# A two-layer decoder step: raw rows transposed ahead of the norm, router logits by token, and a routing table of row numbers for the first 128 places

## The chip, the cores and the metric

The kernel runs on one core of one Trainium2 chip. The metric is the device time of one execution in microseconds (us); lower is better. The engines are TensorE (PE in the rows, PEld for its weight loads), VectorE (DVE), ScalarE (ACT), GpSimd (POOL) and SyncE (SP), which here only issues DMA transfers.

## The reference

One step of a decoder with 2 layers and a model width of 1024, over 512 prompt tokens and 64 sample tokens (8 sequences of 8). Only what the change touches:

```python
def rmsnorm(x, g):
    return x * lax.rsqrt(jnp.mean(x * x, axis=-1, keepdims=True) + RMS_EPS) * g

def mixer_block(x, ...):
    z = rmsnorm(x, norm_g) @ w_in          # 1024 -> 2560: u | q | k | v | g
    ...                                    # pooling mixer on u, retention on q, k, v, gate g
    return x + concat([pool_out, ret_out]) @ w_out

def hier_moe(x, ...):
    hf = rmsnorm(x, norm_g)
    grp_logits = hf @ w_rg + b_rg          # 4 groups
    exp_logits = hf @ w_re + b_re          # 16 experts, 4 in a group
    # best group by logit, the best two experts in it; gates by softmax
    # y = sum over experts e of gates[:, e] * (silu(hf @ w_gate[e]) * (hf @ w_up[e])) @ w_down[e]
    return x + y
```

After the second layer a last RMSNorm gives the outputs. All arrays are float32.

## The kernel before

**Tiling.** The 576 tokens are 5 tiles of 128 (the last, `LAST`, holds the 64 sample tokens). `x` stays on chip, tokens on partitions. A product with float32 accuracy is made of three TensorE passes: each operand is split into a high part, rounded by ScalarE to the fast float32 form, and a low part that VectorE subtracts, and high*high, high*low and low*high are summed. So `hT`, `lT` are the two parts of the transposed activations, `wh`, `wl` those of a weight tile of 128x512 that arrives in `raw`. `w_hi` and `w_lo` make the parts of a weight tile, 56 of them in a layer (steps `s`): 40 of `w_in`, 16 of `w_out`. A step is 14 matmuls of 128x512 (three for each full tile of tokens, two for the last, whose parts lie side by side), for all five tiles of tokens, and TensorE goes through the steps without a pause where nothing is missing. Steps 0 to 2 go tile by tile, since they start while the tiles are still being normed; the last four steps of `w_out` do too.

**Norm ahead of a product** (`norm_root`, `norm_hi` on ScalarE, `norm` and `norm_lo` on VectorE, `transposes` on TensorE). For each tile: ScalarE squares the row and takes the root, VectorE takes the reciprocal and multiplies x by it and by the gain row (`xm` ahead of the mixer and at the end, `xf` ahead of the experts), TensorE transposes the result in two halves of four 128x128 blocks, ScalarE writes the high part and VectorE the low part of each half.

**Banks of w_in.** The products of a group of 512 columns lie in 6 PSUM banks (`ZB`) for 5 tiles; a bank is copied out (`z_evac`) by ScalarE for the tiles LAST, 0, 2, and by VectorE for 1, 3, before the second tile of the next group may use bank 0.

**Routing** (`logits`, `routing`). After the norm ahead of the experts the 20 router logits are formed with the weights (`wrs`, high and low part side by side, 40 columns) as the stationary operand, in two halves of 320 tokens, then turned back to tokens on partitions by five small transposes. VectorE then runs a chain of small operations: best group, best two experts of it, the place of each token in its expert's list (`place_of`, from a matmul with a triangle of ones), and a table that gives for each expert and each place the number of the row. The table is built for all five turns of 128 places (`atslot`, `spread`, ten matmuls, and seven operations after them that end with `pidx` and `tidx`). The normed rows `xf` go to memory (`xn_d`), and GpSimd gathers for each expert the rows by `tidx` with an indirect DMA; after the expert the rows are scattered to `y_d` by `pidx`. Each expert's list here fits the first 128 places, and the code for later turns is jumped over.

**Experts.** 16 experts in order, each 24 matmuls of 128x512 for gate and up, 12 for down, and ten transposes; the weights of experts 0, 1, 2 are loaded during the end of `w_out`; those of expert 3 (`AHEAD`, 3 MB in four transfers) into buffers that the norm and the router still use, so that SyncE waits for the writes of `xn_d` and for the logits ahead of it. Afterwards the rows of `y_d` come back as `back` (ten transfers, two for each tile), and `combine` adds them to `x` with the gates `pgate`.

## Time and profile before

| | |
|---|---|
| median of 3 runs | 933.63 us (933.05 to 934.26) |
| the profiled execution's own time | 933.09 us |
| its span, first to last instruction | 931.3 us |
| TensorE busy | 801.2 us, 86% of the span |
| VectorE busy | 637.5 us, 68% |
| ScalarE busy | 459.7 us, 49% |
| GpSimd busy | 258.9 us, 28% |
| chain that ended last | TensorE 81%, VectorE 10%, DMA 4%, ScalarE 3%, issue 2% |
| moved by DMA | 184.64 MB, mean 198 GB/s |

An engine's busy share is a mean over stages. The two layers are told apart by time: layer 0 ends where the rows of its experts are added (about 447 us), layer 1 about 900 us. The chain that ended last is followed back from the last instruction, at each step to what released it.

### The profile page before, as it was taken

The numbers are of one execution on the slowest core, as the hardware profiler recorded it, in microseconds if no ns is written. First come the engines' busy times: TensorE is split into PE (matmuls) and PEld (weight loads), VectorE is DVE, ScalarE is ACT, GpSimd is POOL, SyncE is SP. The second block draws the span as 40 slices with busy tenths as digits, with TensorE's granted clock in tenths as the row PEclk, the third lists the DMA queues.
The fourth block names the chain that finished last, engine by engine and source line by source line (L and its number), as shares of the span: only waits on it lengthen the run. The fifth ranks groups of instructions, "written<-read, shape, count | busy, mean of one in ns | idle before, by whom it ended". The sixth has DMA issues, their size and how long they took to land.

```text
span 931.3 us, 11658 instructions
## 1 busy us (share of the span) xinstructions
PE 801.2 (86%) x3974; PEld 656.7 (71%) x3974; DVE 637.5 (68%) x1009; ACT 459.7 (49%) x767; POOL 258.9 (28%) x211
## 2 busy tenths in 40 slices
PE   5999999999827999998199999999994499999930
...
GB/s 293 156 69 77 74 72 81 80 135 209 398 145 191 315 315 396 395 347 89 249 83 140 71 73 70 79 112 26 168 376 294 77 313 288 373 387 377 208 132 200
DMA packets 61356, 184.64 MB, mean 198 GB/s; under 512 B 15452, under 2 KB 17756, under 8 KB 52970
## 3 DMA queue, kind: packets, MB, share of 16 engines
...
q14 instruction: 22, 0.18, 0.1%
...
## 4 chain that ended last, share of the span: by engine, by line
PE 81%; DVE 10%; DMA 4%; ACT 3%; issue 2%; SPq 0%; POOLq 0%; ACTq 0%; DVEq 0%
PE ps L368 13%; PE ps L372 10%; PE ps L371 10%; PE ps L1043 10%; PE ps L1045 10%; PE ps L1044 10%; PE ps L1049 3%; PE ps L370 3%; DVE x L1590 2%; PE ps L1225 2%; PE ps L1217 1%; DVE xm L1483 1%; DMA back<-y_d 1%; PE ps L1038 1%; DVE x L1367 1%
## 5 line engine op out<-in xcount | busy, mean ns | idle before, releaser
L368 PE MATMUL ps<-wh,hT 128*128 128x512 f32 x480 | 193.8, 404 | 4.3 <-ACT z L821 2.4
L1498 DVE TENSOR_TENSOR wl<-raw,wh 128x512 fp32r<-128x512 f32 x112 | 95.6, 859 | 112.2 <-ACT wh L811 112.0
L1504 DVE TENSOR_TENSOR gul<-wgu,eh 128x1024 fp32r<-128x1024 f32 x128 | 150.8, 1218 | 10.0 <-ACT eh L836 9.7
L372 PE MATMUL ps<-wh,lT 128*128 128x512 f32 x384 | 151.2, 394 | 0.0
L371 PE MATMUL ps<-wl,hT 128*128 128x512 f32 x384 | 151.1, 393 | 0.0
L811 ACT ACTIVATE wh<-raw 128x512 fp32r<-128x512 f32 x112 | 69.7, 630 | 140.2 <-PE ps L370 111.5
L836 ACT ACTIVATE eh<-wgu 128x1024 fp32r<-128x1024 f32 x128 | 128.9, 1057 | 10.5 <-PE ps L1045 10.5
L1043 PE MATMUL ps<-eh,hgTh 128*128 128x512 f32 x256 | 104.5, 408 | 6.2 <-DVE hgTl L1515 6.2
L368 PEld LDWEIGHTS ps<-wh,hT 128*128 128x128 f32 x480 | 91.0, 190 | 25.5 <-issue 8.0
L1045 PE MATMUL ps<-eh,hgTl 128*128 128x512 f32 x256 | 101.3, 396 | 0.0
L1044 PE MATMUL ps<-gul,hgTh 128*128 128x512 f32 x256 | 101.2, 395 | 0.0
...
L372 PEld LDWEIGHTS ps<-wh,lT 128*128 128x128 f32 x384 | 72.9, 190 | 15.9
L371 PEld LDWEIGHTS ps<-wl,hT 128*128 128x128 f32 x384 | 73.2, 191 | 13.5
L1509 DVE TENSOR_TENSOR dnl<-wdn,eh 128x1024 fp32r<-128x1024 f32 x64 | 75.5, 1222 | 2.5 <-ACT eh L845 1.9
L656 POOL DMA_INDIRECT hg<-xn_d,tidx x32 | 38.0, 1188 | 133.8 <-PE ps L1049 106.2
L845 ACT ACTIVATE eh<-wdn 128x1024 fp32r<-128x1024 f32 x64 | 64.3, 1061 | 0.0
L1043 PEld LDWEIGHTS ps<-eh,hgTh 128*128 128x128 f32 x256 | 48.9, 191 | 17.3 <-DVE hgTl L1515 7.5
L1043 PE MATMUL ps<-eh,actTh 128*128 128x512 f32 x128 | 54.0, 422 | 6.1 <-DVE dnl L1509 6.1
L1045 PEld LDWEIGHTS ps<-eh,hgTl 128*128 128x128 f32 x256 | 48.8, 191 | 10.7
L1044 PEld LDWEIGHTS ps<-gul,hgTh 128*128 128x128 f32 x256 | 49.0, 191 | 9.4
L850 ACT ACTIVATE hgTh<-ps 128x512 fp32r<-128x512 f32 x64 | 34.8, 596 | 40.8 <-PE ps L1049 40.8
...
## 6 DMA issues: line engine op xcount, KB each, us to landing
...
```

Of the source, the lines that this page charges most:

```text
L368: pe.matmul(out, both, w_h, start=first, stop=False)
L371: pe.matmul(out, both, w_l, start=False, stop=False)
L372: return pe.matmul(out, l[:, t * P:(t + 1) * P], w_h, start=False, stop=final)
L811: sc.activation(wh[S % SPL][:, :], raw[S % RAW][:, :], ACT.Copy).then_inc(whi, 1)
L836: sc.activation(eh[p][:, :], gu_pair(wgu, wgu3, e, s, p), ACT.Copy).then_inc(ghi, 1)
L845: sc.activation(eh[4 + k][:, :], dn_chunk(wdn, wdn3, e, s, k), ACT.Copy).then_inc(dhi, 1)
L1043: pe.matmul(out, hi_l, hi_r, start=first, stop=False)
L1044: pe.matmul(out, hi_l, lo_r, start=False, stop=False)
L1045: return pe.matmul(out, lo_l, hi_r, start=False, stop=final)
L1498: ve.tensor_tensor(wl[S % SPL][:, :], raw[S % RAW][:, :], wh[S % SPL][:, :].bitcast(F32), ALU.subtract).then_inc(wlo, 1)
L1504: ve.tensor_tensor(gu_pair(gul, gul3, e, s, p), gu_pair(wgu, wgu3, e, s, p), eh[p][:, :].bitcast(F32), ALU.subtract).then_inc(glo, 1)
L1509: ve.tensor_tensor(dn_chunk(dnl, dnl3, e, s, k), dn_chunk(wdn, wdn3, e, s, k), eh[4 + k][:, :].bitcast(F32), ALU.subtract).then_inc(dlo, 1)
```

## The change

**The norm of the mixer.** TensorE transposes `x` itself (`mix_rows`), so a tile can be transposed as soon as it is there. The gain (`gcol`, one column of 128 numbers for each block) is multiplied into `w_in` while its parts are made, in `w_hi` and `w_lo`; the squares and one root for all tiles (`mix_square`, `mix_root`) run during the steps 3 to 8, and `rstd` is applied where the PSUM banks are copied out (`z_evac`, `z_last`).

**The norm ahead of the experts.** `x` is transposed (`ffn_rows`) into `xT`, plain float32 without a low part. The squares are taken in two halves of the row. The normed rows `xf` (`xn_rows`) are now only for the gather; those of the last tile are made late, in the middle of `routing`. The logits are formed by token, `xT` stationary and the 20 columns of `wr` (with the gain multiplied in) moving, in plain float32, five times 8 matmuls. The bias is multiplied by `rms` in place of dividing the logits (`bias_scale`), and the scale `rstd` comes in only ahead of the two exponentials.

**Routing.** The tests for the best use differences against zero. The table is built for the first 128 places only, as row numbers right away (`name_p` and `name_b`, 20 matmuls of 32 columns, one operation that writes `rowidx`); what later turns need stands in `later_turns`, inside the branch that is not taken here. The last norm is as before. SyncE no longer loads the gain of the mixer's norm.

```diff
-            load_x(0)
-            load_gain(0)
-            for t in range(1, NT):
+            sp.dma_start(gcol[:, :, :, :], a["gcol"]).then_inc(gcol_ld, 16)
+            for t in range(NT):
                 load_x(t)
-                if t - 1 < RAW:
-                    load_raw(0, t - 1)
+                if t < RAW:
+                    load_raw(0, t)
...
-                load_gain(2 * L + 2)
+                if L + 1 == NL:
+                    load_gain(NL)
                 for t in (2, 3, LAST):
                     sp.wait_ge(xn_st[t], 16 * (L + 1))
-                sp.wait_ge(lg_mm, L + 1)
+                sp.wait_ge(lg_mm, 2 * (L + 1))
...
+            def mix_square(L, t):
+                x_there(sc, L, t)
+                sc.activation(xn[0][t][:, :], x[:, t, :], ACT.Square, accum_out=ss[:, t:t + 1]).then_inc(sq_done, 1)
+            def mix_root(L):
+                sc.wait_ge(sq_done, 16 * L + NT)
+                sc.activation(rms[:, :], ss[:, :], ACT.Sqrt, bias=eps[:, 0:1], scale=1.0 / D).then_inc(rms_done, 1)
...
+            def ffn_square(L, t, half):
+                sc.wait_ge(xw, 15 * L + NT * (1 + half) + t + 1)
+                if half == 0 and t >= 3:
+                    sc.wait_ge(s0_st, 64 * (L + 1))
+                cols = slice(512 * half, 512 * half + 512)
+                sc.activation(xn[1][t][:, cols], x[:, t, cols], ACT.Square, accum_out=(ss, ss2)[half][:, t:t + 1]).then_inc(sq_done, 1)
...
+            def ffn_root(L, t):
+                sc.wait_ge(sq_done, 16 * L + 2 * NT + t + 2)
+                sc.activation(rms[:, t:t + 1], ss2[:, t:t + 1], ACT.Sqrt, bias=ssb[:, t:t + 1], scale=1.0 / D).then_inc(rms_done, 1)
+            def ffn_rows(L, t):
+                sc.wait_ge(tr_done, 20 * L + 10 + 2 * t + 1)
+                if t == 0:
+                    sc.wait_ge(s0_st, 64 * (L + 1))
+                sc.activation(xT[:, 0:4, t * P:(t + 1) * P], tr_bank(1, 2 * t).rearrange("p (k c) -> p k c", k=4), ACT.Copy).then_inc(hi_done, 1)
+            def xn_out(L, t):
+                sc.wait_ge(xn_done, NT * L + t + 1)
+                sc.dma_start(xn_d[t * P:(t + 1) * P, :], xn[1][t][:, :]).then_inc(xn_st[t], 16)
...
-                sc.activation(wh[S % SPL][:, :], raw[S % RAW][:, :], ACT.Copy).then_inc(whi, 1)
+                if s < WIN_STEPS:
+                    sc.activation(wh[S % SPL][:, :], raw[S % RAW][:, :], ACT.Copy, scale=gcol[:, 0, L, s % KC:s % KC + 1]).then_inc(whi, 1)
...
+                    if m == LAST or (m == 0 and g == 0):
+                        sc.wait_ge(rstd_done, L + 1)
...
+                    sc.activation(dst, ps[m % ZB][:, :], func, scale=rstd[:, t:t + 1]).then_inc(z_part if t == LAST else zfree[m % ZB], 1)
...
+                table(ACT.Sqrt)
+                for t in range(NT):
+                    mix_hi(L, t)
+                    if L == 0:
+                        for s in ((0, 1), (2,), (), (), ())[t]:
+                            w_hi(0, s)
                 for s in range(RAW, WIN_STEPS + 3):
                     w_hi(L, s)
+                    if s - RAW < NT:
+                        mix_square(L, s - RAW)
+                    if s - RAW == NT:
+                        mix_root(L)
...
-                norm(2 * L + 1)
+                for t in range(NT):
+                    ffn_square(L, t, 0)
+                ffn_first_half(L)
+                for t in range(NT):
+                    if t < LAST:
+                        ffn_square(L, t, 1)
+                        ffn_root(L, t)
+                    ffn_rows(L, t)
+                    if t and t < LAST:
+                        xn_out(L, t - 1)
+                ffn_square(L, LAST, 1)
+                ffn_root(L, LAST)
+                xn_out(L, 3)
                 table(ACT.Exp)
...
-            def logits(L, i):
-                pe.wait_ge(wr_lo, L + 1)
-                pe.wait_ge(lo_done, 10 * (2 * L + 1) + (6, 10)[i])
...
+            def logits(L, t):
+                out = ps[0][:, 20 * t:20 * t + 20] if t < LAST else ps[7][0:NSAMP, 0:20]
+                pe.wait_ge(wr_g, L + 1)
+                pe.wait_ge(hi_done, 15 * L + 10 + t + 1)
                 for k in range(KC):
-                    if k:
-                        pe.matmul(out[0:20, 0:n], wrs[:, k, 0:20], lT[:, k, low], start=False, stop=False)
-                    last = pe.matmul(out[0:40, 0:TOK // 2], wrs[:, k, :], hT[:, k, cols], start=(k == 0), stop=(k == KC - 1))
-                    if k == 0:
-                        pe.matmul(out[0:20, 0:n], wrs[:, k, 0:20], lT[:, k, low], start=False, stop=False)
-                last.then_inc(lgT_mm, 1)
+                    if k == 4:
+                        pe.wait_ge(lo_done, 15 * L + 10 + t + 1)
+                    last = pe.matmul(out, xT[:, k, t * P:t * P + tokens(t)], wr[:, k, :], start=(k == 0), stop=(k == KC - 1))
...
-                for t in range(NT + 2):
-                    if t < NT:
-                        for s in range(2 * KC - SPL, 2 * KC):
-                            wout_mm(L, s, t)
-                    if t == NT + 1:
-                        logits(L, 0)
-                    if t >= 2:
-                        transposes(2 * L + 1, t - 2)
-                logits(L, 1)
...
                 for t in range(NT):
-                    last = pe.transpose(ps[3][:, 40 * t:40 * t + 40], lgT[0:40, t * P:(t + 1) * P], ident[0:40, 0:40])
-                last.then_inc(lg_mm, 1)
+                    for i in range(2 * KC - SPL, 2 * KC - 2):
+                        wout_mm(L, i, t)
+                    if t == LAST:
+                        logits(L, 2)
+                    for i in range(2 * KC - 2, 2 * KC):
+                        wout_mm(L, i, t)
+                    if t:
+                        ffn_rows(L, t - 1)
+                    if t in (2, 3):
+                        logits(L, t - 2)
+                ffn_rows(L, LAST)
+                logits(L, 3)
+                logits(L, LAST)
...
-                pe.wait_ge(tab_ready, L + 1)
                 for i in range(2 * NT):
-                    last = pe.matmul(ps[2][:, 0:NT * 2 * NE], atslot[:, i, :], spread[:, i, :], start=(i == 0), stop=(i == 2 * NT - 1))
+                    if i % NT == 0:
+                        pe.wait_ge(tab_ready, 2 * L + i // NT + 1)
+                    pe.matmul(ps[2][:, 0:2 * NE], atslot[:, i, :], over(name_p[:, i, :], 2), start=(i == 0), stop=False)
+                    last = pe.matmul(ps[2][:, 0:2 * NE], atslot[:, i, :], name_b[:, i, :, :], start=False, stop=(i == 2 * NT - 1))
                 last.then_inc(tab_mm, 1)
...
+            ve.tensor_tensor(name_p[:, :, :], one, c("pair", 2 * NT)[:, :, 0:1].to_broadcast([P, 2 * NT, NE]), ALU.mult)
+            ve.tensor_tensor(name_b[:, :, :, :], over(one, 2, 2), c("block", 2 * NT).unsqueeze(3).to_broadcast([P, 2 * NT, 2, NE]), ALU.mult)
+            ve.wait_ge(pos_mm, L + 1)
+            link(ve.tensor_tensor(picked[:, :, :, :], both[:, :, :, :], over(ps[1][:, 0:NT * NE].rearrange("p (t e) -> p t e", t=NT), 2), ALU.mult))
+            link(ve.tensor_reduce(place_of[:, :], picked[:, :, :, :].rearrange("p k t e -> p (k t) e"), AX.X, ALU.add))
+            for k in range(2):
+                half = slice(NT * k, NT * k + NT)
+                ve.tensor_tensor(atslot[:, half, :], over(c("slot"), NT), place_of[:, half].unsqueeze(2).to_broadcast([P, NT, P]),
+                                 ALU.is_equal).then_inc(tab_ready, 1)
+            link(ve.tensor_reduce(most_f[:, :], ps[1][:, 96:96 + NE], AX.X, ALU.max))
+            xn_rows(L, LAST)
+            link(ve.tensor_tensor(gds[:, :, :], gd[:, :, :], wide(rstd[:, :], 4), ALU.mult))
+            ve.tensor_tensor(col(4), col(2), rstd[:, :], ALU.mult).then_inc(exp_in, 1)
+            ve.wait_ge(tab_mm, L + 1)
+            ve.tensor_scalar(rowidx[:, :, :], ps[2][:, 0:2 * NE].rearrange("p (w e) -> p w e", w=2), float(NO_ROW), None, ALU.add).then_inc(tidx_done, 1)
...
+            def ffn_rows(L, t):
+                ve.wait_ge(tr_done, 20 * L + 10 + 2 * t + 2)
+                ve.tensor_copy(xT[:, 4:8, t * P:(t + 1) * P], tr_bank(1, 2 * t + 1).rearrange("p (k c) -> p k c", k=4)).then_inc(lo_done, 1)
+            def ffn_scale(L, t):
+                ve.wait_ge(rms_done, 6 * L + 2 + t)
...
+            def xn_rows(L, t):
+                if t == 0:
+                    ve.wait_ge(gain_ld, 16 * (L + 1))
+                ve.scalar_tensor_tensor(out=xn[1][t][:, :], in0=x[:, t, :], scalar=rstd[:, t:t + 1], in1=gain[:, :],
+                                        op0=ALU.mult, op1=ALU.mult).then_inc(xn_done, 1)
+            def bias_scale(L):
+                link(ve.tensor_tensor(brms[:, :, :], over(rbias[:, :], NT), rms[:, :].unsqueeze(2).to_broadcast([P, NT, 20]), ALU.mult))
...
-                    norm(2 * L, lambda t, k: combine(L - 1, t, k))
+                    combine(L - 1, 0, 0)
+                    combine(L - 1, 0, 1)
                 else:
-                    norm(0)
+                    ve.wait_ge(gcol_ld, 16)
+                for t in range(NT):
+                    if L and t + 1 < NT:
+                        combine(L - 1, t + 1, 0)
+                    mix_lo(L, t)
+                    if L and t + 1 < NT:
+                        combine(L - 1, t + 1, 1)
+                    if L == 0:
+                        for s in ((0, 1), (2,), (), (), ())[t]:
+                            w_lo(0, s)
+                if L == 0:
                     ve.wait_ge(cst_ld, 32)
                 for s in range(RAW, WIN_STEPS + 4):
                     w_lo(L, s)
+                    if s == RAW + NT + 1:
+                        mix_scale(L)
...
-                norm(2 * L + 1, lambda t, k: None if k else x_add(ve, L, 2, t))
-                routing(ve, L, link, gu_lo)
+                x_add(ve, L, 2, 0)
+                for t in range(3):
+                    x_add(ve, L, 2, t + 1)
+                    ffn_rows(L, t)
+                    ffn_scale(L, t)
+                    xn_rows(L, t)
+                x_add(ve, L, 2, LAST)
+                ffn_rows(L, 3)
+                ffn_rows(L, LAST)
+                ffn_scale(L, 3)
+                xn_rows(L, 3)
+                ffn_scale(L, LAST)
+                bias_scale(L)
+                routing(ve, L, link, gu_lo, xn_rows)
```

How the instructions stand on an engine, before and after, at three places.

VectorE at the start of layer 1, where the experts' rows are added to x (`back_*` are the loaded rows, `xm_*` the normed tile). Before:

```order
L1590 SCALAR_TENSOR_TENSOR x<-back_114,pgate,x 128x1024
L1590 SCALAR_TENSOR_TENSOR x<-back_115,pgate,x 128x1024
L1482 RECIPROCAL rstd<-rms 128x1
L1483 SCALAR_TENSOR_TENSOR xm_169<-x,rstd,gain 128x1024
L1590 SCALAR_TENSOR_TENSOR x<-back_116,pgate,x 128x1024
L1469 TENSOR_TENSOR lT<-ps,hT 128x4x128 x2
```

The same place after the change:

```order
L1706 SCALAR_TENSOR_TENSOR x<-back_116,pgate,x 128x1024
L1561 TENSOR_TENSOR lT<-ps,hT 128x4x128 x2
L1706 SCALAR_TENSOR_TENSOR x<-back_117,pgate,x 128x1024
L1706 SCALAR_TENSOR_TENSOR x<-back_118,pgate,x 128x1024
L1561 TENSOR_TENSOR lT<-ps,hT 128x4x128 x2
```

The reciprocal and the multiplication by `rstd` and the gain have left the stretch; two additions and one pair of low parts for each tile stay.

TensorE at the end of layer 0's `w_out`, without the rows of `w_out` itself (`xf_*` normed tiles; the name ahead of the comma is the moving operand, the other the stationary one). Before, the last rows up to the table:

```order
L1038 MATMUL ps<-cst,xf_177 128x128 x8
...
L1156 MATMUL ps<-hT,wrs 40x320
L1306 MATMUL ps<-cst,lgT 128x40 x5
L1312 MATMUL ps<-taken,tri 128x16 x15
L1315 MATMUL ps<-taken,tri 128x16 x5
L1320 MATMUL ps<-spread,atslot 128x160 x10
```

After the change:

```order
L1225 MATMUL ps<-wr,xT 128x20 x8
L385 MATMUL ps<-wh_62,hT 128x512
L387 MATMUL ps<-wl_66,hT 128x512
L385 MATMUL ps<-wh_63,hT 128x512
L387 MATMUL ps<-wl_67,hT 128x512
L1100 MATMUL ps<-cst,x 128x128 x16
L1225 MATMUL ps<-wr,xT 128x20 x8
L1225 MATMUL ps<-wr,xT 64x20 x8
L1381 MATMUL ps<-taken,tri 128x16 x15
L1385 MATMUL ps<-taken,tri 128x16 x5
```

Three of the five tiles' logits now stand inside the last steps of `w_out`, and behind the last step there are 16 transposes and 16 small matmuls where there were 24 transposes, 32 matmuls of 192 or 320 columns and five small transposes.

VectorE in `routing` of layer 0, from the places to the row numbers (`L1504` and `L1619` are the low parts of expert 0's weights). Before:

```order
L1427 TENSOR_REDUCE place_of<-picked 128x10
...
L1432 TENSOR_TENSOR atslot<-cst,in_turn 128x1280
L1433 TENSOR_TENSOR spread<-hotturn,named 128x1600
...
L1448 TENSOR_SCALAR small_tab<-tmpf 128x80
L1449 TENSOR_TENSOR tidx<-small_tab,tmpf 128x80
L1504 TENSOR_TENSOR gul_74<-wgu_68,eh_121 128x1024
```

After the change:

```order
L1492 TENSOR_REDUCE place_of<-picked 128x10
L1495 TENSOR_TENSOR atslot<-cst,place_of 128x640 x2
L1497 TENSOR_REDUCE most_f<-ps 128x1
L1584 SCALAR_TENSOR_TENSOR xf_186<-x,rstd,gain 128x1024
L1499 TENSOR_TENSOR gds<-gd,rstd 128x20
L1500 TENSOR_TENSOR small<-small,rstd 128x5
L1503 TENSOR_SCALAR rowidx<-ps 128x32
```

Fifteen operations from the places to the row numbers have become seven, and one of the seven is the last tile of normed rows, which before stood well ahead of `routing`.

## Rows read from the trace of the kernel before

**Rows 1.** Stretches: engine busy us and instructions, granted clock, DMA share, GB/s

```profile
28.20:124.00 95.80, 94.04 (x424) 75.82 (x423) 43.83 (x62) 29.70 (x63) 43.83 (x35) 1.00 0.35 97
...
230.60:246.90 16.30, 15.66 (x80) 12.52 (x78) 13.77 (x22) 8.68 (x19) 0.00 (x0) 1.00 1.01 413
246.90:284.60 37.70, 12.76 (x92) 9.55 (x91) 26.11 (x69) 12.71 (x22) 7.83 (x7) 0.68 0.53 196
284.60:437.50 152.90, 148.30 (x716) 122.45 (x716) 142.72 (x169) 123.40 (x169) 37.18 (x27) 0.99 0.82 305
```

**Rows 2.** Timeline of the start: start us, us, engine, line, operation, count

```profile
4.65 1.06 ACT L776 ACTIVATE xm<-x 128x1024 f32<-128x1024 f32 x1 [2.40 <-DMA x<-in_x_prompt]
...
7.13 1.28 DVE L1483 SCALAR_TENSOR_TENSOR xm<-x,rstd,gain 128x1024 f32<-128x1024 f32 x1
8.18 1.06 ACT L776 ACTIVATE xm<-x 128x1024 f32<-128x1024 f32 x1 [2.06 <-DMA x<-in_x_prompt]
...
11.09 1.28 DVE L1469 TENSOR_TENSOR lT<-ps,hT 128x512 fp32r<-128x512 f32 x2
...
13.88 0.77 PE L368 MATMUL ps<-wh,hT 128*128 128x512 f32 x1 [0.62 <-DVE wl L1498]
...
18.83 0.48 PE L368 MATMUL ps<-wh,hT 128*128 128x512 f32 x1
```

**Rows 3.** Timeline of TensorE where step 3 begins, layer 0

```profile
28.21 0.39 PE L368 MATMUL ps<-wh,hT 128*128 128x512 f32 x1
28.44 0.39 PE L371 MATMUL ps<-wl,hT 128*128 128x512 f32 x1
```

**Rows 4.** Timeline of layer 1's start

```profile
455.65 1.29 DVE L1590 SCALAR_TENSOR_TENSOR x<-back,pgate,x 128x1024 f32<-128x1024 f32 x1 [1.76 <-DMA back<-y_d]
...
458.48 1.94 PE L1038 MATMUL ps<-cst,xm 128*128 128x128 f32 x8 [16.36 <-DVE xm L1483]
...
477.14 1.03 PE L1038 MATMUL ps<-cst,xm 128*128 128x128 f32 x8
...
481.52 0.39 PE L368 MATMUL ps<-wh,hT 128*128 128x512 f32 x1
```

**Rows 5.** Timeline where the second group of w_in begins, layer 0

```profile
44.77 1.08 ACT L821 ACTIVATE unat<-ps 128x512 f32<-128x512 f32 x2
...
45.51 0.47 PE L368 MATMUL ps<-wh,hT 128*128 128x512 f32 x1 [0.59 <-ACT unat L821]
```

**Rows 6.** Line L889: ScalarE copies of a PSUM bank with a scale for each partition

```profile
L889 ACT ACTIVATE hP<-ps,pscale x8: 687/687/689, 62.8 to 564.6; 128x512 fp32r<-128x512 f32 x8
```

**Rows 7.** Line L821: who waited for these copies, us and times

```profile
  PE ps L368: 3.5, 6
```

**Rows 8.** Timeline of layer 0 from the last tiles of w_out to expert 0

```profile
249.61 1.57 PE L1038 MATMUL ps<-cst,xf 128*128 128x128 f32 x8 [2.67 <-DVE xf L1483]
...
260.63 0.17 DVE L1392 TENSOR_REDUCE small<-lg 128x5 f32<-128x20 f32 x1
...
265.48 0.24 DVE L1411 TENSOR_TENSOR taken<-picked,cst 128x80 bf16<-128x80 f32 x1
...
268.71 1.49 DVE L1432 TENSOR_TENSOR atslot<-cst,in_turn 128x1280 bf16<-128x1280 f32 x1
...
274.87 0.24 DVE L1449 TENSOR_TENSOR tidx<-small_tab,tmpf 128x80 uint32<-128x80 f32 x1
...
275.98 1.24 POOL L656 DMA_INDIRECT hg<-xn_d,tidx  x1 [13.18 <-DVE tidx L1449]
...
280.59 1.97 PE L1049 MATMUL ps<-cst,hg 128*128 128x128 f32 x8 [7.08 <-DMA hg<-xn_d,tidx]
...
284.64 0.79 PE L1043 MATMUL ps<-eh,hgTh 128*128 128x512 f32 x1 [2.09 <-DVE hgTl L1515]
```

**Rows 9.** The chain that ended last: 16 float32 matmuls with 128x128 weights, 8 columns each

```profile
183.06 1.69 PE ps L1217 x16
```

**Rows 10.** Writes of the last outputs (L1005), issue to landing, ns and us

```profile
L1005 ACTq DMA_DIRECT2D out_y_prompt<-xm x4: 338/342/351, 913.3 to 926.0; - x4
...
DMA to landing us min/median/max: 2.6/2.8/3.8
```

**Rows 11.** The gathers (L656), issue to landing over both layers

```profile
DMA to landing us min/median/max: 4.7/7.5/8.8
```

**Rows 12.** The loads of back (L593), issue to landing

```profile
DMA to landing us min/median/max: 3.4/7.4/11.4
```

294 lines of the change are left out of this document (153 added, 141 removed).

## The prediction

> **What bounds the kernel now.** I read the stretches first [rows 1]. From 28.2 to 124 us and from 284.6 to 437.5 us TensorE works for 97 to 98% of the time: there it sets the pace, and a change of other engines' work is worth nothing unless it makes TensorE wait. In 230.6 to 246.9 us it is at 15.7 of 16.3 us. The stretch behind it is different: of 37.7 us TensorE works 12.8, at a granted clock of 0.68. This is where the norm, the router and the first gather stand one behind the other, once in each layer. The timelines show the other two places, the start [rows 2] and the start of layer 1 [rows 4]. The last norm is a fourth, but its order on each engine stays, so it adds nothing. The sum is therefore over two starts and two routing stretches, less what the steps of `w_in` lose.
>
> **The start of layer 0.** Tile 0 of x is there at 4.65 us (its square starts), the normed tile is ready at 7.13 + 1.28 = 8.4, and only then can TensorE transpose it; the first product starts at 13.88 and step 3 at 28.21 [rows 2, 3]. Afterwards x itself is transposed. One small load (`gcol`) goes ahead, so say tile 0 at 5.2. The gain row's 512 KB leave the queue, so tile 1, which landed by 8.2, comes at about 7.3. Transposes at the low clock take 1.94 for eight [rows 4]: tile 0 to 7.2, tile 1 to 9.3. The parts of weight tile 0 stand behind tile 0's parts, ready about 9.4, and the first product starts there, 4.4 earlier. The third weight tile's low part stands behind the low parts of tile 1 (1.28 for two [rows 2]), at about 12.0, when TensorE needs it. From then on it is TensorE's work as before: two tiles' starts stood 2.95 apart. Step 3 starts at about 24.0. Gain **4.2**. If the loads are the limit, only half: 2; if everything shifts by the first product, 4.4.
>
> **The start of layer 1.** The additions for tile 1 wait for `back` until 455.65, and step 3 starts at 481.52 [rows 4]. In between VectorE has per tile two additions (2.4), the multiplication (1.3), a reciprocal (0.2) and a pair of low parts (1.3): 5.1. Without the two middle ones it is 3.7 for a tile. TensorE has 1.03 of transposes and nine matmuls, 2.05 at the cadence of 0.227 us for one [rows 3], so 3.1 at the full clock: VectorE stays the slower, but for the first tile, where TensorE is at the low clock. Walking it through: additions to 456.9, low parts of tile 0 to 458.2, then one tile in about 3.7 to 4.4, last addition at 471.5, last transposes 472.5, tiles 3 and 4 of the products 2.05 + 1.36, step 3 at 475.9. Gain **5.6**. The ten loads of `back` land 3.4 to 11.4 after their issue [rows 12], a spread of 8 us over five tiles, so they are not in the way of a pace of 3.7. Bounds: 3.5 if the low clock lasts a tile longer, 6.5 if it is four times 1.5 and a little.
>
> **The steps of w_in.** The scale in the bank copies: ScalarE's copy with a scale per partition takes 0.687 [rows 6] against 0.54 to 0.6 now (two in 1.08) [rows 5], and TensorE waits for the second of two such copies, 0.59 us [rows 5], in all 3.5 us at six places [rows 7]. Two copies 0.09 longer make each wait 0.18 longer: loss **1.1**. The scale in `w_hi` (0.09 more) and in `w_lo` (one row of the same kind is 1.28 for 1024 columns, so 0.65 to 0.7 for 512, as now) lies under steps of 14 x 0.227 = 3.2 us, and so do the squares moved to steps 3 to 7: ScalarE then has 0.7 + 1.3 = 2.0 of 3.2. Without that cover each square would cost its 1.3. The root is ready two steps before the first bank is to be copied.
>
> **The routing stretch.** TensorE's last steps start at 230.6. Now 56 matmuls (12.7), eight transposes for a tile (0.9) and the logits. Float32 matmuls with 128x128 weights and few columns: 16 in 1.69 [rows 9], so 0.85 for a tile's eight. From below a transposing group of eight costs no less; from above it would be the double, at the low clock. Placed in the order shown, the last `w_out` matmul ends at 249.1, the last addition to x at 250.5, the last transposes at 251.5, the last logits at 253.2. There VectorE has been behind: additions 1.35, copy, copy, `xf` of tile 3 (1.28), two reciprocals, the bias, two additions of the logits, done at 254.6. Before, this point is 260.63 [rows 8], because TensorE waited 2.67 for a normed tile and then did 32 wide matmuls, half of them at the low clock. Gain so far 6.0.
>
> From there to `taken`: before 260.63 to 265.72 with 23 operations, now 20 at 0.21 and a few longer ones, 4.5: 259.1. From there to `place_of`: 0.4 + 0.3 + 0.5 + 0.7 = 2.0. `atslot` in halves costs its 1.49 once [rows 8], `spread` (1.8) and nine of the small operations are gone. But behind `atslot` stands `xf` of the last tile: most_f 0.2, then 1.28, so the row is ready at 264.1, and `rowidx` at 264.6, against `tidx` at 275.1. That is 10.5 earlier.
>
> **The new wait.** The gather needs `xn_d` complete. Before, all normed rows were made ahead of the logits, so the write lay far ahead of the gather. Now it is issued at 264.1. Writes of 512 KB with nothing else going on take 2.6 to 3.8, median 2.8 [rows 10]: 267.0. The gather starts 0.87 behind its release, as now (275.11 to 275.98), at 267.9. Queued behind the write are GpSimd's gathers and, on SyncE, the four loads for expert 3, 3 MB, which wait for the same semaphore. So these start together with the first gather. Before, they were released by the logits' end, some 15 us ahead of the gather, and that gather took 275.98 to 280.59, 4.6 [rows 8]; over both layers gathers take 4.7 to 8.8, median 7.5 [rows 11]. I take 7.5, since the median is that of gathers beside weight loads. So the rows are there at 275.4 instead of 280.59: gain **5.2** in layer 0. Expert 0 then takes its 4.05 as before [rows 8], the high and low parts of its weights being ready by 271.7. In layer 1 the gain row of the last norm is loaded at the moment of the last `xn_d` write, since SyncE waits for all `xf` ahead of it; 512 KB beside it cost about 1.0: gain **4.2**.
>
> The Trainium skill (DMA: Bandwidth & Descriptors, Anatomy of one DMA) gives a fixed 2.0 us and the bytes at 436 per ns for one transfer: an estimate of 3.2 us for this write. The trace's median for the same thing is 2.8 [rows 10]. By the page the gain would be 0.8 us smaller over two layers; the sum goes by the row.
>
> **Sum.** 4.2 + 5.6 - 1.1 + 5.2 + 4.2 = 18.1 us. The profiled execution took 933.09, so 915.0; the median of the runs is 0.5 above it: **915.5 us**. The experts' loops, 153 us each, neither gain nor lose.
>
> **Rivals.**
> 1. *The gather is not slowed.* The rows of a gather may get their share beside the loads: it takes 4.7, and the write in layer 1 isn't slowed either. Then 2 x 2.8 + 1.0 = 6.6 more: 909. For it: the loads' first bytes and the gather's start within a microsecond of each other, and 512 KB are small. Against: the `xn_d` writes beside loads and the gathers inside the loop are all slowed.
> 2. *The starts give less.* The loads at the start (x and three weight tiles) and the low clock in layer 1 hold TensorE back, or VectorE's chain ahead of the logits, which has some 20 us of work in 23, slips by a microsecond or two. Half of both starts gone (4.9) and 1 in each routing stretch: 922.
> 3. *Slower: the two trips to memory in a row.* The write of the last `xf` and the gather that needs it now stand on the path. Each may take as long as the longest landing of 512 KB in the trace, 11.4 [rows 12]. Then rows come at 264.1 + 11.4 + 0.9 + 11.4 = 287.8, 7.2 later than before in each layer, and with the starts' gain of 8.7 the time is 939. It decides from a sum of 19.9 us for both trips; I expect 10.3. Against it: the 11.4 is a load last of ten in a queue, and at 264 us nothing else is queued.
> 4. *No change.* Transposing x earlier could be of no use if the weights' parts came last at both starts, and routing's saving went into the wait for `xn_d`. That wants a trip sum of about 16 and starts of nothing: 933.
>
> **How the numbers follow.** Chances: forecast 0.50, rival 1 0.26, rival 2 0.17, no change 0.03, rival 3 0.04. The forecast's own range is 912 to 919 (start 2 to 4.4, layer 1 3.5 to 6.5, gather 6.5 to 8.8 with each layer). The range 908 to 922 takes in rivals 1 and 2. A measurement tells some 0.2% (1.9 us) from no change: faster 0.93, within 0.03, slower 0.04.
>
> **What the profile after would show.** Step 3 at about 24 us; TensorE's share of the first 28 us up. The bank waits six times 0.77 instead of 0.59. The logits 8 in 0.85 and the first reduce at 254.6. `rowidx` ten us ahead of the old `tidx`, but the first gather released by the landing of `xn_d`, not by VectorE, about 268, and its landing 7 to 8 us later, with wgu and wdn loads under way. In layer 1 VectorE's additions without a pause from 455.65 less the shift, 3.7 for a tile. The prediction is wrong if the gather starts at 265.5 (the write doesn't hold it), if its landing is 4.7, if VectorE falls behind TensorE's logits by more than 2 us, or if TensorE waits in the steps 3 to 10 of a layer for `wl` or `rstd`.

## The result, and the profile after

The changed kernel took **927.17 us** (median of 8 runs, 924.59 to 933.80), the kernel before in the same session 934.14 (8 runs, 933.05 to 935.56): ratio **0.9937**, 95% interval 0.9909 to 0.9965. The sign of the forecast is right, its size is not: 7.0 us were won where 18.1 had been forecast, and the time lies 5 us above the upper end of the range. The profiled execution took 927.14, with a span of 925.3 against 931.3.

The stretches of the changed kernel come first (same columns as [rows 1], same places of the program; the last row is layer 1's experts).

```profile
23.00:119.00 96.00, 93.69 (x423) 75.61 (x423) 44.07 (x63) 36.88 (x72) 43.67 (x35) 1.00 0.35 97
226.10:243.50 17.40, 17.19 (x103) 14.45 (x101) 12.45 (x20) 9.52 (x27) 0.00 (x0) 1.00 0.99 399
243.50:280.10 36.60, 14.09 (x123) 12.31 (x123) 21.19 (x56) 10.26 (x17) 8.49 (x7) 0.63 0.50 181
280.10:439.53 159.43, 153.24 (x728) 125.89 (x728) 144.37 (x170) 124.31 (x171) 41.82 (x28) 0.98 0.79 296
729.49:890.98 161.49, 155.31 (x728) 127.48 (x728) 144.74 (x170) 124.87 (x171) 37.44 (x27) 0.96 0.77 286
```

From the last steps of `w_out` to expert 0 it was 16.3 + 37.7 = 54.0 us [rows 1] and is 17.4 + 36.6 = 54.0. The stretch that should have become some 5 us shorter is as long as it was. TensorE works 10% more in it (17.19 + 14.09 = 31.3 us against 15.66 + 12.76 = 28.4), and its granted clock in the second part went from 0.68 to 0.63.

Next the two starts (timeline; they answer to [rows 2 to 4]): the first product and step 3 of layer 0, then the first additions and step 3 of layer 1.

```profile
9.49 0.78 PE L385 MATMUL ps<-wh,hT 128*128 128x512 f32 x1
...
23.06 0.39 PE L385 MATMUL ps<-wh,hT 128*128 128x512 f32 x1
...
447.14 2.67 DVE L1706 SCALAR_TENSOR_TENSOR x<-back,pgate,x 128x1024 f32<-128x1024 f32 x2 [5.10 <-DMA back<-y_d]
...
471.97 0.39 PE L385 MATMUL ps<-wh,hT 128*128 128x512 f32 x1
```

Step 3 of layer 0 stands at 23.06, before at 28.21: 5.15 won. In layer 1 it comes 24.83 behind the first additions, before 30.30 (451.22 to 481.52): 5.47 won. Twelve kernels of this study have these two starts, and their profiles differ: step 3 of layer 0 stands between 22.89 and 24.32 (once at 26.92), that of layer 1 comes 24.83 to 26.43 behind the first additions. This profile has the shortest of the twelve starts of layer 1. In the steps behind them, line L857 (the bank copies, now with a scale) has these users, to be read beside [rows 7]:

```profile
L857 ACT ACTIVATE z<-ps,rstd x28: 670/684/693, 68.1 to 613.2; 128x512 f32<-128x512 f32 x28
...
  PE ps L385: 4.6, 6
```

And the way to expert 0 in layer 0 (timeline, to be read beside [rows 8]):

```profile
253.97 0.18 DVE L1464 TENSOR_REDUCE small<-lg 128x5 f32<-128x20 f32 x1
...
258.17 0.24 DVE L1478 TENSOR_TENSOR taken<-ohg,ing 128x80 bf16<-128x80 f32 x1
...
261.89 1.28 DVE L1584 SCALAR_TENSOR_TENSOR xf<-x,rstd,gain 128x1024 f32<-128x1024 f32 x1
...
263.20 0.33 ACTq L830 DMA_DIRECT2D xn_d<-xf  x1
263.38 0.18 DVE L1503 TENSOR_SCALAR rowidx<-ps 128x32 uint32<-128x32 f32 x1
...
265.95 0.80 SPq L504 DMA_DIRECT2D wgu<-in_gate_up  x2
266.75 1.90 POOL L673 DMA_INDIRECT hg<-xn_d,rowidx  x1 [10.23 <-DMA xn_d<-xf]
266.79 1.36 SPq L511 DMA_DIRECT2D wdn<-in_w_down  x2
...
276.05 1.97 PE L1122 MATMUL ps<-cst,hg 128*128 128x128 f32 x8 [13.78 <-DMA hg<-xn_d,rowidx]
...
280.11 0.80 PE L1116 MATMUL ps<-eh,hgTh 128*128 128x512 f32 x1 [2.09 <-DVE hgTl L1630]
```

I count from the high part of the last weight tile of `w_out` (ScalarE's last `wh` of the layer), here and before:

```profile
226.12 0.63 ACT L847 ACTIVATE wh<-raw 128x512 fp32r<-128x512 f32 x1 [2.54 <-PE ps L387]
```

```profile
230.58 0.63 ACT L811 ACTIVATE wh<-raw 128x512 fp32r<-128x512 f32 x1 [2.54 <-PE ps L370]
```

From there the first reduce comes at 27.85 (before 30.05), the row numbers at 37.4 (before 44.5), the gather starts at 40.6 (before 45.4), and its rows are there at 49.93 (before 50.01). So 7.1 us were won up to the row numbers, 2.3 went into the wait for `xn_d<-xf`, and the gather itself, 9.30 us against 4.61, took the rest. Layer 1 is the same picture, counted from the same place (675.10, before 683.84): the first reduce at 27.0 (before 30.2), the row numbers at 36.6 (44.7), the gather at 41.8 (45.5), its rows at 50.3 (50.0). There the gather starts at 716.94 and lands at 725.43, 8.49. So the routing stretch, which should have given 5.2 and 4.2 us, gave 0.1 and -0.3.

### The profile page after: what moved, and what is told of

It reads as the page before. It is cut to its first block, busy times and chain, and to the rows that moved or that the text cites. A ratio compares the mean times of both kernels' runs of the same rounds, so it can differ in the third digit from the quotient of the medians.

```text
span 925.3 us, 11832 instructions
## 1 busy us (share of the span) xinstructions
PE 805.1 (87%) x4080; PEld 664.6 (72%) x4080; DVE 616.4 (67%) x961; ACT 464.1 (50%) x767; POOL 264.2 (29%) x211
## 4 chain that ended last, share of the span: by engine, by line
PE 84%; DVE 7%; DMA 5%; ACT 2%; issue 1%; SPq 0%; POOLq 0%; ACTq 0%
PE ps L385 14%; PE ps L389 10%; PE ps L388 10%; PE ps L1116 10%; PE ps L1117 10%; PE ps L1118 10%; PE ps L1122 3%; PE ps L387 3%; DMA hg<-xn_d,rowidx 2%; PE ps L1100 2%; PE ps L1293 2%; PE ps L1285 1%; DMA back<-y_d 1%; PE ps L1225 1%; PE ps L1250 1%
## 5 line engine op out<-in xcount | busy, mean ns | idle before, releaser
L1619 DVE TENSOR_TENSOR gul<-wgu,eh 128x1024 fp32r<-128x1024 f32 x128 | 150.9, 1217 | 15.0 <-ACT eh L872 14.5
L1610 DVE SCALAR_TENSOR_TENSOR wl<-raw,gcol,wh 128x512 fp32r<-128x512 f32 x80 | 75.9, 953 | 82.8 <-ACT wh L845 82.6
L682 POOL DMA_INDIRECT y_d<-y,rowidx x32 | 53.4, 1670 | 141.8 <-DVE y L1637 141.8
L845 ACT ACTIVATE wh<-raw,gcol 128x512 fp32r<-128x512 f32 x80 | 57.6, 723 | 63.1 <-PE ps L387 49.8
L388 PEld LDWEIGHTS ps<-wl,hT 128*128 128x128 f32 x384 | 72.6, 189 | 13.2
L673 POOL DMA_INDIRECT hg<-xn_d,rowidx x32 | 38.5, 1203 | 137.5 <-PE ps L1122 113.4
L1116 PEld LDWEIGHTS ps<-eh,hgTh 128*128 128x128 f32 x256 | 49.7, 194 | 17.4 <-DVE hgTl L1630 7.5
L1122 PE MATMUL ps<-cst,hg 128*128 128x128 f32 x256 | 35.0, 282 | 28.8 <-DMA hg<-xn_d,rowidx 28.8
```

The lines of the kernel that those rows point to most:

```text
L388: pe.matmul(out, both, w_l, start=False, stop=False)
L1116: pe.matmul(out, hi_l, hi_r, start=first, stop=False)
L1122: last = pe.transpose(ps[1 + k // 4][:, (k % 4) * P:(k % 4 + 1) * P], hg[s][:, k * P:(k + 1) * P], ident)
L1610: ve.scalar_tensor_tensor(out=wl[S % SPL][:, :], in0=raw[S % RAW][:, :], scalar=gcol[:, 0, L, s % KC:s % KC + 1], in1=wh[S % SPL][:, :].bi ...
L1619: ve.tensor_tensor(gu_pair(gul, gul3, e, s, p), gu_pair(wgu, wgu3, e, s, p), eh[p][:, :].bitcast(F32), ALU.subtract).then_inc(glo, 1)
```

## The experiments

Each was timed in five rounds (the doubled logits in three) against the kernel before on the same chip; the ratio is to the kernel before, with its 95% interval (its median was 934.0 to 934.6 in these sessions). "Below the changed kernel" means below the 927.17 of the first session. The loads meant below are those of expert 3's weights, 3 MB.

**The logits' price.** Each logits matmul done twice:

```
-                for k in range(KC):
+                for k in [*range(KC), *range(KC)]:
...
                     last = pe.matmul(out, xT[:, k, ...], wr[:, k, :], ...)
```

> The changed kernel with each logits matmul done twice (the second set replaces the first in the bank, the result stays the same). My prediction priced eight of them at 0.85 us, the trace of the changed kernel shows 1.70. If 1.70 is the cost and TensorE's chain of last steps, transposes and logits sets the time up to the first reduce: the last two tiles' logits can't be hidden by waits for VectorE and ScalarE, so 1.7 for each tile that stands on the path, +3.4 to +8.5 in a layer, +7 to +17 in all (934 to 944). If the wait for VectorE's additions set it, as I took in the prediction: at most the last tile's 1.7 in each layer, +3.4 (930.5).

Measured: **959.63** us, ratio 1.0268 (1.0236 to 1.0299): +32 against the changed kernel, nearly twice my highest number. The rows of TensorE in the doubled kernel say why:

```profile
237.77 3.65 PE L1225 MATMUL ps<-wr,xT 128*128 128x20 f32 x32
...
245.00 3.65 PE L1225 MATMUL ps<-wr,xT 128*128 128x20 f32 x32
...
249.52 6.75 PE L1225 MATMUL ps<-wr,xT 128*128 128x20 f32 x32
```

Sixteen instructions take 3.65. In the changed kernel a row of eight is busy for 1.86, and 1.70 pass from its start (236.53) to that of the matmul behind it (238.23); so this agrees. But the third such group takes 6.75: the granted clock has fallen from 1.00 to 0.50 (from 2.4 to 1.2 GHz) while TensorE was busy all the time, with matmuls of 20 columns. The windows from 250 to 254 us of this kernel:

```profile
250.00:254.00 4.00, 4.00 (x21) 4.00 (x20) 0.00 (x0) 0.00 (x0) 0.00 (x0) 0.50 0.00 0
```

The opposite edit, half of the logits. It also moves the wait for the second half of a tile's transposes ahead of the first matmul:

```
-                for k in range(KC):
-                    if k == 4:
-                        pe.wait_ge(lo_done, 15 * L + 10 + t + 1)
...
+                pe.wait_ge(lo_done, 15 * L + 10 + t + 1)
+                for k in range(0, KC, 2):
```

> The changed kernel, but only every second of the eight 128-row pieces of x goes into the logits (the other half of the router's sum is left out; the tokens are spread over the experts otherwise, but every expert's product has the same size). Four logits matmuls then take what I had taken for eight, 0.85 us. Theory A (my sum was off by the price of these matmuls, and TensorE's chain sets the time up to the first reduce): the stretch up to the first reduce is 3.8 us shorter in each layer, as forecast; since the late write then is released by the same chain, all of it arrives at expert 0: -7 to -8, about 920. Rival B (VectorE's additions, squares and copies set that point as well): -1 to -2 in a layer, 923 to 925.

Measured: **920.18** us, ratio 0.9864 (0.9841 to 0.9888), 7.0 below the changed kernel. Theory A holds: `taken` is there 22.9 us behind the first transposes of x for the router in both layers; in the changed kernel it was 26.5 and 25.6. The first reduce shows it best. These are this kernel's last `wh` and first reduce, in layer 0 and in layer 1:

```profile
227.18 0.63 ACT L847 ACTIVATE wh<-raw 128x512 fp32r<-128x512 f32 x1 [2.54 <-PE ps L387]
251.42 0.17 DVE L1463 TENSOR_REDUCE small<-lg 128x5 f32<-128x20 f32 x1
...
672.46 0.63 ACT L847 ACTIVATE wh<-raw 128x512 fp32r<-128x512 f32 x1 [2.54 <-PE ps L387]
696.70 0.17 DVE L1463 TENSOR_REDUCE small<-lg 128x5 f32<-128x20 f32 x1
```

It comes at 24.24 in both layers, 5.8 and 6.0 us earlier than in the kernel before. My prediction had 6.0. With the price that I had assumed, the rest of that step comes out. Layer 0 of the changed kernel also has a fall of the clock at this place; its window first, then this kernel's:

```profile
246.00:250.00 4.00, 4.00 (x19) 3.32 (x19) 1.37 (x2) 0.60 (x1) 0.00 (x0) 0.57 0.15 24
```

```profile
246.00:250.00 4.00, 3.30 (x32) 2.93 (x30) 3.34 (x6) 2.10 (x5) 0.00 (x0) 1.00 0.73 210
```

In the changed kernel the clock is at 0.57 on average over these 4 us, right behind two groups of logits; with half of them it stays at 1.00. Layer 1 of the changed kernel has no such fall, and there half of the logits won 2.8 us, against 3.6 in layer 0. So these four matmuls of each tile cost 2.8 us a layer by themselves, and the fall another 0.8. That the logits bring the fall isn't shown: the kernel before has one at this place too (0.79 and 0.78 in the 4 us from 248 and from 252). Of the 7.0 us, 6.4 are these two stretches; the rest is, roughly, that this profile has no second fall in layer 1's experts (1.9, see below), less a later start of layer 0 (1.1).

**The gather and what runs beside it.** SyncE waits for the first gather before it issues the loads:

```
                 sp.wait_ge(lg_mm, 2 * (L + 1))
+                sp.wait_ge(gat[0], 16 * used(L, 0, 0))
                 load_gu(L, AHEAD, 0)
```

> The changed kernel, but SyncE issues the loads of expert 3's weights (3 MB) only once the first gather has landed. Theory A (the gather is slow because these loads run beside it): the gather takes 4.7 us, as in the kernel before, instead of 9.3 and 8.5; expert 0 starts 4.2 us earlier in each layer; against the changed kernel -8 us (about 919), against the kernel before 0.985. Rival B (the gather is slow because its rows were written just ahead of it, or because of where it stands on its queue): it still takes 8.5 to 9.3, and the time stays within 1 us of the changed kernel (927). Rival C (expert 3's weights are then late): the gain is eaten by a wait of TensorE for the parts of expert 3's weights, 927 or more; the loads have 3 experts, 28 us, ahead of them, so I hold it unlikely.

Measured: **923.02** us, ratio 0.9886 (0.9865 to 0.9908), 4.2 below the changed kernel.

```profile
267.09 1.89 POOL L674 DMA_INDIRECT hg<-xn_d,rowidx  x1 [10.23 <-DMA xn_d<-xf]
...
272.29 1.97 PE L1123 MATMUL ps<-cst,hg 128*128 128x128 f32 x8 [9.68 <-DMA hg<-xn_d,rowidx]
...
272.32 0.81 SPq L504 DMA_DIRECT2D wgu<-in_gate_up  x2
```

The gather takes 5.20 instead of 9.30 (in layer 1 5.44 instead of 8.49): 7.1 us less over the two layers. Rival B falls. Rival C too, no wait for expert 3's weights appears. That the median moved by 4.2 and not by 7.1 comes from elsewhere, as far as the two profiled executions show it (923.51 and 927.14, each close to its median). This one has the later starts:

```profile
24.20 0.39 PE L385 MATMUL ps<-wh,hT 128*128 128x512 f32 x1
...
471.88 0.39 PE L385 MATMUL ps<-wh,hT 128*128 128x512 f32 x1
```

These are step 3 of both layers, 1.1 us later than in the changed kernel in layer 0 and, at 26.43 behind the first additions (445.45), 1.6 later in layer 1, in code that the edit doesn't touch. The experts don't explain it: layer 0's have a second fall of the clock here, 161.80 us from expert 0 to the last scatter where the changed kernel had 159.42, but layer 1's have none, 159.50 against 161.49.

The last tile's row made earlier:

```
                 bias_scale(L)
+                xn_rows(L, LAST)
                 routing(ve, L, link, gu_lo, xn_rows)
...
             link(ve.tensor_reduce(most_f[:, :], ps[1][:, 96:96 + NE], AX.X, ALU.max))
-            xn_rows(L, LAST)
```

> The changed kernel, but VectorE makes the last tile's normed row ahead of the logits' additions and the routing, not behind the table. The write to memory is then issued some 9 us earlier and has landed by the time the row numbers are there, and the loads of expert 3's weights, released by the same landing, start 9 us ahead of the gather instead of together with it. VectorE's chain gets 1.3 us longer ahead of the routing and 1.3 shorter behind the table. Theory A (both trips on the path and the collision with the loads cost what was saved): the gather starts about 0.9 us behind the row numbers, 265.5 instead of 266.75 in layer 0, and takes 4.7 to 6 us instead of 9.3; expert 0 4.5 to 6 us earlier in a layer; against the changed kernel -9 to -12, so 915 to 918. Rival B (the gather is slow by itself): only the 1.2 us of the start are won, 2 in both layers: 925.

Measured: **915.99** us, ratio 0.9811 (0.9788 to 0.9833), 11.2 below the changed kernel, inside the expected 9 to 12. The gather is now released by VectorE, as in the kernel before:

```profile
264.85 1.09 POOL L673 DMA_INDIRECT hg<-xn_d,rowidx  x1 [7.95 <-DVE rowidx L1502]
```

It takes 4.83 in layer 0 and 6.83 in layer 1, where the loads were issued at 703.37 and the gather at 707.66. Both edits together:

> The changed kernel with the last tile's normed row made ahead of the logits' additions and the loads of expert 3's weights behind the first gather: both edits together. With the early row alone the first gather took 4.83 us in layer 0 but 6.83 in layer 1, where those loads were issued only 4.3 us ahead of it (the write that releases them ran beside the gain row's load). Theory A (these loads are what is left in layer 1's gather): it takes 4.7 in both layers, -2 against the early row alone: 914. Rival B (layer 1's gather is slow for another reason): no change, 916. Rival C (the loads, now some 6 to 11 us later, are late for expert 3): slower than 916, with TensorE waiting for the parts of expert 3's weights.

Measured: **912.33** us, ratio 0.9778 (0.9761 to 0.9796), 3.7 below the early row alone where 2 was expected. The gathers take 4.62 and 4.14, layer 1's by these two rows of the timeline (the second is TensorE's first weight load from the gathered rows), so Theory A holds. About 2 of the 3.7 are something else: the profile of the early row alone has a second fall in layer 1's experts (161.50 us), this one has not (159.35):

```profile
708.06 1.09 POOL L674 DMA_INDIRECT hg<-xn_d,rowidx x1 [7.13 <-DVE rowidx L1503]
...
712.20 0.93 PEld L1123 LDWEIGHTS ps<-cst,hg 128*128 128x128 f32 x5 [5.31 <-DMA hg<-xn_d,rowidx]
```

**The parts by themselves.** The kernel before with the table alone:

```
+            ve.tensor_tensor(name_p[:, :, :], one, c("pair", 2 * NT)[:, :, 0:1]...)
+            ve.tensor_tensor(name_b[:, :, :, :], over(one, 2, 2), c("block", 2 * NT)...)
...
+            ve.tensor_scalar(rowidx[:, :, :], ps[2][:, 0:2 * NE]..., float(NO_ROW), None, ALU.add)...
...
-            ve.tensor_tensor(tidx[:, :], small_tab[:, :], tmpf[:, :], ALU.add).then_inc(tidx_done, 1)
```

> The kernel before, with only the change of the table (row numbers of the first 128 places alone; the longer table is made behind the experts, if it is wanted at all). Norm, logits and their order are those of before, so the normed rows are written far ahead of the gather. Theory A (the table's gain is real and it is the late write and the loads beside the gather that took it away in the changed kernel): the row numbers come 4.4 us earlier (23 small operations fewer or shorter, spread gone), the gather still takes 4.6 to 5, so the time is -4.4 in each layer, -8.8 in all, ratio 0.9906, some 924.8 and so no slower than the whole change. Rival B (an earlier gather meets the loads of expert 3's weights anyway, since those are released at the end of the logits): the gather takes 7 or more, the time is within 3 us of the kernel before.

Measured: **927.04** us, ratio 0.9924 (0.9900 to 0.9948): as fast as the whole change. From the end of `taken` to the gather 10.26 became 5.53 in layer 0 and 10.24 became 5.51 in layer 1, and the gathers took 4.59 and 4.43:

```profile
269.89 0.19 DVE L1446 TENSOR_SCALAR rowidx<-ps 128x32 uint32<-128x32 f32 x1 [0.53 <-PE ps L1328]
...
270.94 1.29 POOL L661 DMA_INDIRECT hg<-xn_d,rowidx  x1 [8.46 <-DVE rowidx L1446]
```

The 9.5 us of the trace became 7.3 in the median; layer 1's experts have the second fall here. The loads, released at the logits' end as before, are out of the way. Then the kernel before with the mixer's norm alone:

```
-                transposes(2 * L, 0)
+                mix_rows(L, 0)
...
+                    sc.activation(wh[S % SPL][:, :], raw[S % RAW][:, :], ACT.Copy, scale=gcol[:, L, s % KC:s % KC + 1])...
...
+                    sc.activation(dst, ps[m % ZB][:, :], func, scale=rstd[:, t:t + 1])...
```

> The kernel before with only the first norm of each layer changed: x itself is transposed, the gain is in the parts of the weight tiles, the root's scale in the copies of the banks; norm ahead of the router, logits and table stay as before. From the profiles of before and after: start of layer 0 5.15 us shorter, start of layer 1 5.47 shorter, the steps 0.7 and 0.9 longer. Theory A (the starts' gains are gains of the whole): -9.0, ratio 0.9903, some 925.3. Rival B (an earlier start is given back at the next place where TensorE waits, or by a fall of its clock in the experts): between -4 and -7. Rival C (the longer bank copies cost more once the rest is as before): less than -7 with the loss in the steps, over 2 a layer.

Measured: **925.82** us, ratio 0.9911 (0.9896 to 0.9927), -8.6 where -9.0 was expected. In its profile the last `wh` of `w_out` comes 4.4 earlier in layer 0 and, counted from layer 0's last scatter, 3.7 in layer 1; another 1.4 are in layer 0's logits, which the edit doesn't touch and which have no fall of the clock here. And both:

> The kernel before with the first norm of each layer and the table changed, but not the norm ahead of the router and not the logits: the whole change without its middle part. If the parts add up: -9.0 for the norm and -7.3 as measured for the table alone (two gathers 4.75 earlier each in the trace), so -16.3, about 918, ratio 0.9825. Against the changed kernel (927.2) that is -9: the middle part, with the late write and the loads beside the gather that it brings, would then be worth a loss of 9. If instead the middle part is a gain, as I took in the prediction (6.0 us a layer up to the first reduce), this kernel is slower than 918, or no faster than the changed one.

Measured: **919.07** us, ratio 0.9829 (0.9811 to 0.9847): -15.3, the parts add up (7.3 + 8.6 = 15.9), although its profiled execution has the latest start of the twelve (step 3 of layer 0 at 26.92). This kernel is 8.1 us faster than the changed one, which has the middle part (transposes of x for the router, logits by token, root later) on top.

**Both wrong terms taken out.**

> The changed kernel with both of the terms that my sum had wrong put as it had them: half of the logits' matmuls (so 0.85 us a tile as I had priced them; half of the router's sum is left out) and the loads of expert 3's weights behind the first gather. If these two are the whole of the error, their measured effects add up, -7.0 and -4.1 from 927.2: 916, and my forecast was 915.5. If the two overlap or a third cause is at work: 919 or more.

Measured: **913.78** us, ratio 0.9781 (0.9766 to 0.9797), 13.4 below the changed kernel. The logits are now as the sum had them, and the first reduce comes at 24.24 again in both layers. The gathers are better than in the sum, 4.84 and 5.27 where it had 7.5, 4.9 us over both layers. So the 1.7 below my forecast don't mean that these two terms are the whole of the error: with gathers of 7.5 this kernel would be at 918.7 (an estimate), 3 above it. In the profile the logits give 6.4 and the gathers 7.7 against the changed kernel, and later starts take back 1.7.

**TensorE's clock at expert 0.** In every kernel so far the clock stands at 0.50 when expert 0 begins. In the early row's kernel with the loads behind, TensorE got work while it waited (in a free bank, 32 times, then 16):

```
+                for i in range(FILL):
+                    pe.matmul(ps[3][:, 0:P], ident, ident, start=True, stop=True)
                 pe.wait_ge(gat[0], 16 * used(L, 0, 0))
                 rows_t(0).then_inc(t_mm, 1)
```

> The same as the early row with the loads behind the gather, and TensorE does 32 transposes of the constant identity into a free bank behind the table's matmuls, where it waits some 7.5 us for the first gather. They take part in no result. In all kernels so far the granted clock stands at 0.50 from the router's end up to about 4 us into expert 0; the eight transposes of the gathered rows take 1.97 us there against 0.87 at the full clock. Theory A (the clock rises with work and holds over a short wait): the 32 take about 5.6 us and end ahead of the gather; the transposes take 0.9 instead of 1.97, the first 4 us of expert 0 cost 2 us less: -2.5 to -3 in each layer, -5 to -6 in all, 908 to 909. Rival B (the clock has fallen again by the time the rows are there, or the dummy work draws a fall later): within 1.5 of the same kernel without them. Rival C (the dummy work runs past the landing): it delays the transposes by what it overruns, the time is equal or slower.

Measured: **914.80** us, ratio 0.9799 (0.9775 to 0.9823), no gain over 912.33: rival C. The 32 (plain matmuls, my text calls them transposes) overran the landing:

```profile
264.82 9.61 PE L1398 MATMUL ps<-cst 128*128 128x128 f32 x64
274.27 1.04 PE L1124 MATMUL ps<-cst,hg 128*128 128x128 f32 x8
...
277.40 0.50 PE L1118 MATMUL ps<-eh,hgTh 128*128 128x512 f32 x1 [2.09 <-DVE hgTl L1633]
```

The mechanism is there all the same: the rows' transposes take 1.04, not 1.97, and expert 0's first matmul is at the full clock; the stretch of the experts took 157.44 and 157.60.

With 16 in place of 32 (`FILL = 16`):

> As the last kernel (early row, loads behind the gather, TensorE busy ahead of it), with 16 plain matmuls of 128 columns instead of 32. The 32 took 9.6 us (at half the clock for the first 4.5) and ran 3.6 us past the landing of the gather in layer 0, 3.3 in layer 1. Theory (their overrun ate the gain of the clock): 16 take about 5.6 us, end at or just before the landing; the rows' transposes take 1.04 instead of 1.97 and the experts' stretch is 2 us shorter as measured with the 32, so -3 in a layer, -6 against the same kernel without them (912.3): 906.5. Rival: the clock falls back or rises too late, 910 to 912.

Measured: **910.19** us, ratio 0.9747 (0.9732 to 0.9763): 2.1 won, not 6, which is where the rival had it (910 to 912). The 16 ended in time, but in this profile the clock fell again behind the wait of 2.44 us for `hgTl` (windows around expert 0's first matmul):

```profile
269.11:271.11 2.00, 0.00 (x1) 0.01 (x1) 1.94 (x3) 0.76 (x2) 1.27 (x1) 1.00 0.91 328
271.11:273.11 2.00, 2.00 (x6) 1.58 (x7) 0.00 (x0) 0.00 (x0) 0.00 (x0) 0.62 0.98 389
273.11:275.11 2.00, 2.00 (x7) 1.56 (x6) 0.29 (x1) 1.06 (x1) 0.00 (x0) 0.52 0.95 385
```

So the cost of the low clock stayed for another 4 us.

And with more of them behind expert 0 (`busy(n)` is the loop above, n times):

```
                     rows_t(q).then_inc(t_mm, 1)
+                if first(e):
+                    busy(2)
...
                 act_t().then_inc(at_mm, 1)
+                if first(e):
+                    busy(4)
```

> As the kernel with 16, and TensorE does 2 and 4 such matmuls more in its two waits between expert 0 and expert 1 (0.57 and 1.01 us). In 5 of the 18 layers profiled so far without dummy work the granted clock fell to 0.50 a second time right behind these waits, for some 3.5 us, and the stretch from expert 0 to the last scatter then took 161.5 to 161.9 instead of 158.9 to 159.5. Theory A (the waits behind expert 0 let the clock fall): the fall doesn't occur, the runs lie within 3 us of each other, and the median is the same or up to 1.3 lower than with 16 alone. Rival B (the fall has nothing to do with these waits): same spread and same median; if the additions overrun the waits, up to 0.5 a layer slower.

Measured: **906.59** us (905.99 to 907.50), ratio **0.9707** (0.9694 to 0.9720), the fastest kernel of the study, and the runs lie within 1.5 us. Theory A's spread holds; the median fell by 3.6 against the kernel with 16 alone, where at most 1.3 was expected. That it is the waits behind expert 0 that this kernel closed is argued, not shown: of the 22 layers profiled without such work, 6 had the second fall, all behind these waits, some 12 us into the experts, and in this kernel's profile there is none in layer 0 and only one at expert 0's beginning in layer 1. The profile of the changed kernel shows one, in layer 1 behind such waits:

```profile
740.48 0.50 PE L1116 MATMUL ps<-eh,hgTh 128*128 128x512 f32 x1 [1.01 <-DVE hgTl L1630]
...
742.00 0.63 PE L1118 MATMUL ps<-eh,hgTl 128*128 128x512 f32 x1
...
744.92 0.40 PE L1116 MATMUL ps<-eh,hgTh 128*128 128x512 f32 x1
```

## Why the prediction was wrong, step by step

- **Start of layer 0**, forecast 4.2: 5.15 in the profile. First product forecast at 9.4, it is 9.49; the full clock came earlier than I had walked it. Of the twelve profiles with this start eleven give 3.9 to 5.3 and one 1.3. Right.
- **Start of layer 1**, forecast 5.6: 5.47, but this is the best of the twelve, which begin at 3.9. The mechanism is right, and the size in this profile is in part luck. The mixer's norm alone, with 4.4 and 3.7 us up to the end of `w_out`, shows both starts less the loss: 8.1 where the sum had 8.7.
- **The steps of w_in**, forecast a loss of 1.1: 0.69 and 0.89, so 1.6. The copies take 0.684, and TensorE waited 4.6 at the six places in place of 3.5, the 1.1 of the forecast. Right; where the other 0.5 went is open.
- **Logits.** This step failed: "Float32 matmuls with 128x128 weights and few columns: 16 in 1.69 [rows 9], so 0.85 for a tile's eight." The row's x16 counts records, not instructions: the loop behind L1217 runs over 8 sequences, and its plain float32 matmuls stand in the trace twice each. Over the whole kernel L1225 shows it in its own count, x160 for 2 layers of 5 tiles of 8 matmuls:

```profile
L1225 PE MATMUL ps<-wr,xT x160: 181/266/266, 236.5 to 701.7; 128*128 128x20 f32 x128, 128*64 128x20 f32 x32
```

  Transposes of float32 stand there once each (x8 for eight). A tile's eight logits matmuls cost 1.70, not 0.85. The first reduce came 2.2 us earlier in layer 0 and 3.2 in layer 1, not 6.0. In layer 0 a fall of the clock has a part of 0.8 in it, which the sum didn't have either. With half of the matmuls, so at the assumed price, the first reduce came 5.8 and 6.0 earlier, and the time was 7.0 us lower.
- **Table.** The routing stretch behind `taken` and the table went as worked out; alone it is worth 7.3 us. With the logits' loss of 3.8 and 2.8, the row numbers came 7.1 and 8.1 earlier, not 10.5; the table's own part, 4.9 in each layer, is 0.4 above the forecast.
- **The write of the last xf**, forecast 2.9 in layer 0: it landed 2.6 after its issue. In layer 1, with the gain row loaded at the same moment (711.36), 4.7: forecast 1.0 more, it was 2.1 more. Right in kind, short by 1.
- **The gather beside the loads**, taken at 7.5 as the median of [rows 11]: 9.30 and 8.49. This is the second failed step. The mechanism was right, the size was not: the median was over gathers that meet some load or other, while this one starts within a microsecond of 3 MB. The 8.8 at the upper end of that row was the nearer one. With the loads behind it, it takes 5.2 and 5.4.
- **"The experts' loops, 153 us each, neither gain nor lose"**: from expert 0 to the last scatter 159.05 and 159.44 became 159.42 and 161.49; the 2 us in layer 1 are the second fall of the clock, a cost that the sum put at nothing. The runs of the changed kernel, 924.6 to 933.8, follow their mean granted clock (0.938 at 924.59, 0.926 at 933.80).

By the sum, the forecast was missed by 11.7 us. In the profiled execution the logits account for 6.6 of it (3.8 and 2.8), the gathers for 2.8 (1.8 and 1.0), the experts' stretches for 2.4, the write in layer 1 for 1.0 and the steps of `w_in` for 0.5; the table and the starts give 1.6 back. The two edits by themselves gave 7.0 and 4.2, together 13.4. In the traces their own effects do add up: 6.4 for the logits and 7.1 for the gathers, 13.5. The single medians hide it, since starts and falls of the clock differ from one profiled execution to the next by 1 to 2 us in a layer. What is open is what sets these: why a start is early or late, and in which layer the second fall comes.

No rival allowed for a wrong price of the logits. The slower one (two trips in a row) was right that write and gather stand on the path: 2.6 + 9.3 = 11.9 in layer 0 and 4.7 + 8.5 = 13.2 in layer 1, where I expected 10.3 and 11.3, and 19.9 would have decided.

The rule for one transfer that I had weighed (the Trainium skill, DMA: Bandwidth & Descriptors, Anatomy of one DMA) would have given an estimate of 3.2 us for the write. That section fits it to transfers that GpSimd issues, and this write is issued by ScalarE. The trace shows 2.6 with nothing beside it, so the row of the trace was the better price here.
